# Eleven row slots for the gathered experts, and one weight buffer where there were two

## Chip, cores and metric

The kernel runs on one core of a Trainium2 chip. The metric is the device time of one launch in microseconds, the median of several runs.

## The reference

One inference step of a small diffusion backbone in float32: 384 tokens (128 of a prompt, 256 of a sample), width 1024, two layers. Layer 0 mixes tokens with an RG-LRU, layer 1 with gated linear attention (GLA); adaLN scales and shifts come from a conditioning vector. After each mixer stands PEER, a channel mixer that picks, for each token and each of 8 heads, 16 of 16384 experts by product keys, and reads from a table one row u and one row v of 1024 numbers for each:

```python
def block(args):
    xb, eb, gb = args
    ub = jnp.take(u_tab, eb, axis=0)
    act = jax.nn.gelu(jnp.einsum('td,thkd->thk', xb, ub).astype(jnp.float32))
    vb = jnp.take(v_tab, eb, axis=0)
    return jnp.einsum('thk,thkd->td', (gb * act).astype(vb.dtype), vb)
```

The GLA mixer projects each token to q, k, v, an output gate and decays (`xm @ w_in`), runs a decayed state over chunks of 64 tokens in both directions, and projects back (`@ w_out`).

## The kernel before, in words

**Order of the work.** An opening computes the adaLN vectors and the RG-LRU of layer 0. Then one long loop (`peer`, lines 1181, 776 and 1642) goes through both layers' PEER: 6 tiles of 128 tokens (prompt, sample 0, sample 1, for each layer), 8 heads each, so 48 blocks (`NBLK`) of 16 experts, and 4 steps of 4 experts per block: 192 steps (`NSLOT`). The GLA mixer of layer 1 and the expert queries of layer 1 are not a stage of their own; they run in slots beside those steps (`beside`, line 1176). The prompt's GLA begins at step 32 (`BASE[0]`) beside the tiles of the sample in layer 0, the sample's at step 96 (`BASE[1]`) beside the prompt's tile in layer 1. Each piece has a slot number written by hand; `slots.run(step)` runs what is due after the step's own work. "Step 5" of a stage is the one with slot number 5 after its `BASE`.

**One expert row.** POOL (line 441) issues an indirect DMA that gathers, for 128 tokens, one row of u and v: 8 KB for each of 128 partitions, 1.049 MB, into one of `RS` = 10 slots (`row`, line 268) in `arena`. It first waits until `row_free` says that the slot's last user is done. DVE multiplies u by the token and sums (line 1651), ACT applies gelu (L798), DVE weighs (L1662), ACT makes a diagonal matrix of the weights (L805), and PE multiplies the diagonal by v into PSUM (`pair`, line 1225, L1233) and frees two slots per pair. PE does the pairs of a step first, then parts of the expert queries of layer 0 (L1207) or the slots' mixer work. At the end of each tile (`turn`, line 1240; every 32 steps) PE waits until ACT has copied the sums out (L563), clears PSUM (L1222) and turns the tile (L1255) before it takes new rows.

**The weights.** The query weights of layer 0 (`wq0`, 8 items), the GLA weights (`gla0` for the prompt, `gla1` for the sample, 16 items each: 0 to 3 q and k, 4 to 7 v, 8 to 11 gates, 12 to 15 output) and the queries of layer 1 (`wq1`, `wq2`) are 56 items of 1 MB in the order of `ITEMS` (line 81). SP loads them one after the other (line 411) into two buffers in turn, `w_flat[0]` in `area` and `w_flat[1]` at the start of `spare` (line 264), the part of `arena` behind the ten slots. Item m is issued when PE has finished with item m - 2 (line 406). On PE, `wait_item` (line 944) waits for the item in front of the first product that needs it: `columns` (L982) for q, k, gates and output, `values` (L999) for v, `late_queries` (L1164), `queries` (L1207). An item of q and k serves two products, `q_and_k(2j)` and `q_and_k(2j+1)`. Their slots, and those of the value products (two per item in the sample's stage, one in the prompt's), are these:

```python
V_SLOTS = ((8, 9, 10, 11), (8, 9, 9, 10, 10, 11, 12, 13))
QK_SLOTS = (3, 4, 5, 6, 6, 7, 7, 8)
```

Gates stand in slots 14, 15, 18 and 19 (one item each), the output products in slots 22 to 25 (one item each, two products), and the queries of layer 1 three steps apart. The expert queries of layer 0 use one item in the first two steps of each block. SP also loads the keys of layer 1 (line 416) behind the second item of `wq1` and of `wq2`. POOL issues gathers only.

Of the kernel before, what the change touches and what calls it, by code (L numbers as in the profile page):

```python
# [13 lines left out]
D = 1024  # L14
# [20 lines left out]
PH, NK, TOPK = 8, 128, 16  # L35
NEXP = NK * NK
NB = NT * PH
RS, DS = 10, 8
HALF = P // 2
PARTS = [range(4 * i, 4 * i + 4) for i in range(4)]  # L40
NBLK = DEPTH * NB
# [4 lines left out]
AW = 3120  # L46
# [20 lines left out]
for _j in range(4, 8):  # L67
# [13 lines left out]
ITEMS = ([("wq0", h) for h in range(PH)] + [("gla0", j) for j in range(16)] + [("wq1", h) for h in range(PH)]  # L81
         + [("gla1", j) for j in range(16)] + [("wq2", h) for h in range(PH)])
ITEM_AT = {item: m for m, item in enumerate(ITEMS)}


V_SLOTS = ((8, 9, 10, 11), (8, 9, 9, 10, 10, 11, 12, 13))
# [115 lines left out]
def build(nc, x_t, pos_t, vecs, ident_d, mask_d, iota_d, keys_t, ada_w, peer_wq, peer_uv, rg_w_in,  # L202
          rg_wa, rg_wi, rg_w_out, gla_w_in, gla_w_z, w_alpha, state_gla, gla_w_out, y_t, st_rg, st_gla):
    ctx = ExitStack()
    with ctx:
# [55 lines left out]
        ada_rows = small[:, 0:512]  # L261
        gdec = small[:, 768:768 + 2 * HEADS * NCH]
        mask = sb("mask", [P, 8 * CH], U32)
        spare = arena[:, RS * 2 * D:8 * AW]
        gap = area[:, 3072:3840]

        xn1, sq1 = cols(A[0]), cols(A[2])
# [92 lines left out]
        @block.sync  # L360
        def _(sp):
            def wait_used(k):

                name, j = SEQ[k]
                if name == "ada":
                    sp.wait_ge(sem("ada_used"), j + 1)
                else:
                    sp.wait_ge(sem(name + "_mm"), 2 * j + 2)

            sources = {"rg_in": rg_w_in, "rg_out": rg_w_out}  # L370

            def stream(first, end):

                for k in range(first, end):
                    name, j = SEQ[k]
                    w = ada_w[j // 24] if name == "ada" else sources[name]
                    n = j % 24 if name == "ada" else (j + 4) % 8 if name == "rg_in" else j
                    if BEFORE[k] is not None:
                        wait_used(BEFORE[k])
                    sp.dma_start(slab_flat[SLOT[k]], w[n]).then_inc(slab_in[SLOT[k]], 16)  # L380

            def wait_item(m):

                kind, j = ITEMS[m]
                s = int(kind[-1])
                if kind[:2] == "wq":
                    sp.wait_ge(sem(f"q_mm{s}"), 2 * (j + 1))
                elif j < 4:
                    sp.wait_ge(sem("qk_mm"), 2 * j + 2 + s * BY_PROMPT["qk_mm"])
                elif j < 8:  # L390
                    sp.wait_ge(sem("v_mm"), TILES[s] * (j - 3) + s * BY_PROMPT["v_mm"])
                elif j < 12:
                    sp.wait_ge(sem("g_mm"), 2 * (j - 8) + 2 + s * BY_PROMPT["g_mm"])
                else:
                    sp.wait_ge(sem("out_mm"), 2 * (j - 12) + 2 + s * BY_PROMPT["out_mm"])

            stream(0, len(SEQ))
            wait_used(LAST_IN[SLABS])
            sp.dma_start(keys[:, :], keys_t[:, 0, :]).then_inc(keys_in, 16)
            wait_used(LAST_IN[SLABS + 1])  # L400
            sp.wait_ge(sem("rg_gate_mm"), 32)
            for m, (kind, j) in enumerate(ITEMS):
                if m == 1:
                    sp.wait_ge(sem("rg_out_mm"), C)
                elif m >= 2:
                    wait_item(m - 2)
                if kind[:2] == "wq":
                    source = peer_wq[min(int(kind[-1]), 1), j]
                else:
                    source = gla_w_in[j] if j < 12 else gla_w_out[j - 12]  # L410
                sp.dma_start(w_flat[m % 2], source).then_inc(w_in[m % 2], 16)
                if (kind, j) == ("wq0", 1):
                    sp.wait_ge(sem("rg_fin"), 1)
                    sp.dma_start(st_rg, rgfin[:, :, :]).then_inc(sem("st_rg_out"), 16)
                elif kind in ("wq1", "wq2") and j == 1:
                    sp.dma_start(keys[:, :], keys_t[:, 1, :]).then_inc(keys_in, 16)
            for i in range(4):
                sp.wait_ge(sem("y_ready"), 2 * (i + 1))
                sp.dma_start(y_t[:, 2 * i:2 * i + 2, :], hT[:, 2 * i:2 * i + 2, :]).then_inc(sem("y_out"), 16)
            sp.wait_ge(sem("y_out"), 64)  # L420
            sp.wait_ge(sem("st_rg_out"), 16)
            for i in range(2):
                sp.wait_ge(sem(f"st_gla_out{i}"), 16 * HEADS)
# [3 lines left out]
        def _(pool):  # L427
# [6 lines left out]
            for b in range(NBLK):  # L434
                pool.wait_ge(sem("idx_ready"), b + 1)
                rows = idx[b % 4]
                for j in range(TOPK):
                    n = b * TOPK + j
                    if n >= RS:
                        pool.wait_ge(row_free, n - RS + 1)  # L440
                    pool.indirect_dma_start(  # L441
                        row[n % RS], None, rows_of,
                        bass.IndirectOffsetOnAxis(ap=rows[:, j:j + 1], axis=0)).then_inc(row_in[n % RS], 16)
# [427 lines left out]
        def _(pe):  # L871
# [72 lines left out]
            def wait_item(kind, j):  # L944

                m = ITEM_AT[kind, j]
                pe.wait_ge(w_in[m % 2], 16 * (m // 2 + 1))
                return w_slab[m % 2]

            def gla(s):  # L950
                n, at, nt = WIDTH[s], BASE[s], TILES[s]
# [229 lines left out]
            def peer():  # L1181
# [17 lines left out]
                                  start=True, stop=True).then_inc(sem("first_s_mm"), 1)  # L1199

                def queries(h, half, chunks=range(C), t0=0):
                    slab_ = w_slab[h % 2]
                    if half == 0 and chunks[0] == 0:
                        wait_item("wq0", h)
                        pe.wait_ge(sem("s_ev0"), 2 * h)
# [641 lines left out]
```

## Time and profile before

| | us |
|---|---|
| median of 3 runs | 2517.98 (2516.24 to 2521.56) |
| the profiled execution | 2520.77 |
| its span | 2519.0 |
| PE busy | 1745.2 |
| DVE busy | 1540.6 |
| POOL busy | 876.5 |
| ACT busy | 647.1 |
| bytes moved | 940.29 MB, mean 373 GB/s |

The span is the time from the first to the last instruction; the execution has 1.8 us around it. Busy times of the engines overlap. Rows of the trace are quoted below in groups; in a timeline a row is a run of like instructions, with the idle time of the engine ahead of it and what ended that in brackets.

### The profile page before, as it was taken

Reading aid. Unit: us, or ns where it says so; the run is one execution under the profiler, and the core shown is the slowest. Engines: PE = TensorE matmul, PEld = TensorE weight load, DVE = VectorE, ACT = ScalarE, POOL = GpSimd, SP = SyncE. Lnnn points to the kernel's source line nnn. Section 1 sums busy time; section 2 is a strip of 40 time slices with the busy share of each in tenths; the row PEclk is TensorE's granted clock in tenths of the full one; section 3 lists DMA queues with packets and bytes.
Section 4 is the critical chain, followed back from the end, with each engine's and each line's share of the span. In section 5 each row is a group of like instructions: output and inputs, shape, how many; then the busy total and the mean of one; then the engine's idle time right before and its main releaser. Section 6 shows DMA issues by size and latency. Waiting matters only on the chain.

```text
span 2519.0 us, 28267 instructions
## 1 busy us (share of the span) xinstructions
PE 1745.2 (69%) x10284; PEld 866.4 (34%) x10284; DVE 1540.6 (61%) x3946; ACT 647.1 (26%) x1689; POOL 876.5 (35%) x775
## 2 busy tenths in 40 slices
PE   5998877765676865765665788986566765655555
PEld 2555622321343432322221455653333321211112
DVE  2225556667676766557576677765356667667753
ACT  2260312221341432221212352332112221122111
POOL 0000243534343333334444343233134444344441
PEclk8999898987788887777777799998688878677777
DMA  8883599999799999799999799989589999799994
GB/s 299 334 314 154 225 421 421 421 421 411 317 421 421 413 403 418 313 421 421 421 421 417 311 411 417 370 363 417 205 339 421 416 421 419 318 421 421 421 420 194
DMA packets 136361, 940.29 MB, mean 373 GB/s; under 512 B 19168, under 2 KB 21728, under 8 KB 22432
## 3 DMA queue, kind: packets, MB, share of 16 engines
q0 software_dynamic: 110592, 805.36, 77.6%
q1 hardware_dynamic: 17856, 126.37, 12.6%
q10 hardware_dynamic: 7776, 6.77, 0.9%
q8 instruction: 82, 1.34, 0.2%
q14 instruction: 55, 0.45, 0.0%
HBM read 935.81 MB, written 2.63 MB: 373 GB/s over the span
## 4 chain that ended last, share of the span: by engine, by line
DMA 38%; PE 35%; DVE 13%; POOL 4%; issue 4%; ACT 4%; ACTq 1%; SPq 0%; DVEq 0%
DMA arena<-in_peer_uv,idx 36%; PE psum L1233 16%; DVE arena L1651 6%; POOL arena L441 4%; PE psum L929 4%; PE psum L982 3%; PE psum L1164 2%; PE psum L1207 2%; ACT diag L805 2%; PE psum L1255 2%; PE psum L1222 2%; PE psum L894 1%; PE psum L916 1%; PE psum L1319 1%; DMA slabs<-in_ada_w 1%
## 5 line engine op out<-in xcount | busy, mean ns | idle before, releaser
L441 POOL DMA_INDIRECT arena<-in_peer_uv,idx x768 | 872.5, 1136 | 1598.1 <-PE psum L1233 1123.1
L1233 PE MATMUL psum<-arena,diag 64*64 64x512 f32 x6144 | 957.1, 775 | 651.7 <-ACT diag L805 651.6
L1651 DVE SCALAR_TENSOR_TENSOR arena<-arena,xtok 128x1024 f32<-128x1024 f32 x768 | 928.9, 1224 | 668.0 <-DMA arena<-in_peer_uv,idx 660.5
L1233 PEld LDWEIGHTS psum<-arena,diag 64*64 64x64 f32 x6144 | 303.9, 174 | 1230.3 <-issue 1228.6
L798 ACT ACTIVATE gelu<-dots 128x4 f32<-128x4 f32 x192 | 39.5, 206 | 1111.9 <-DVE arena L1651 1111.7
L805 ACT ACTIVATE diag<-ident,wts 128x64 f32<-128x64 f32 x768 | 204.3, 336 | 366.8 <-DVE wts L1662 366.8
L929 PE MATMUL psum<-arena,slabs 128*128 128x384 f32 x288 | 98.4, 502 | 9.8 <-DVE arena L1748 6.5
L798 ACT ACT_TABLE_LOAD x61 | 78.3, 1283 | 1.1
L1222 PE MATMUL psum<-zrow 1*128 1x512 f32 x48 | 40.8, 1022 | 52.0 <-ACT slabs L563 52.0
L929 PEld LDWEIGHTS psum<-arena,slabs 128*128 128x128 f32 x288 | 55.9, 196 | 49.7 <-issue 13.3
L1651 DVE DVE_READ_ACCUMULATOR arena<-arena,xtok 128x1 f32 x768 | 62.9, 82 | 0.0
L554 ACT ACT_TABLE_LOAD x45 | 57.7, 1283 | 0.8
L894 PE MATMUL psum<-slabs,cond 128*2 128x256 f32 x528 | 50.2, 401 | 9.9 <-DMA slabs<-in_ada_w 9.9
L1662 DVE TENSOR_TENSOR wts<-gelu,ex 128x4 f32<-128x4 f32 x192 | 30.5, 159 | 38.9 <-ACT gelu L798 38.9
L982 PE MATMUL psum<-area 128*128 128x128 f32 (+1 forms) x256 | 46.3, 338 | 4.2 <-DVE keys L1538 4.2
L1164 PE MATMUL psum<-area 128*128 128x128 f32 (+1 forms) x256 | 45.7, 338 | 3.0 <-ACT xtok L752 3.0
L1164 PE MATMUL psum<-area,arena 128*128 128x128 f32 (+1 forms) x256 | 46.6, 342 | 0.0
L982 PE MATMUL psum<-area,arena 128*128 128x128 f32 (+1 forms) x256 | 44.9, 331 | 0.9 <-DMA arena<-in_gla_w_in 0.9
L1255 PEld LDWEIGHTS psum<-ident,slabs 128*128 128x128 f32 x192 | 41.4, 332 | 10.5 <-issue 7.5
L1164 PEld LDWEIGHTS psum<-area 128*128 128x128 f32 x256 | 39.8, 195 | 12.9 <-issue 6.1
L1255 PE MATMUL psum<-ident,slabs 128*128 128x64 f32 x192 | 42.5, 423 | 2.1 <-ACT slabs L563 2.1
L1164 PEld LDWEIGHTS psum<-area,arena 128*128 128x128 f32 x256 | 40.5, 198 | 9.9 <-issue 6.0
(267 smaller groups left out, 1828.3 us busy)
## 6 DMA issues: line engine op xcount, KB each, us to landing
slabs<-in_ada_w SPq DMA_DIRECT2D x33, 1024.0 KB, 7.6
area<-in_peer_wq SPq DMA_DIRECT2D x12, 1024.0 KB
arena<-in_peer_wq SPq DMA_DIRECT2D x12, 1024.0 KB
arena<-in_peer_uv,idx POOLq DMA_INDIRECT x768, 11.5
area<-in_gla_w_in SPq DMA_DIRECT2D x12, 1024.0 KB
arena<-in_gla_w_in SPq DMA_DIRECT2D x12, 1024.0 KB
keys<-in_ada_w SPq DMA_DIRECT2D x8, 1024.0 KB, 8.3
area<-in_ada_w SPq DMA_DIRECT2D x7, 1024.0 KB, 7.0
```

Of the source, the lines that this page charges most:

```text
L441: pool.indirect_dma_start(row[n % RS], None, rows_of, bass.IndirectOffsetOnAxis(ap=rows[:, j:j + 1], axis=0)).then_inc(row_in[n % RS], 16)
L554: act.activation(ex[b % 4][:, :], sc[b % 4][:, :], ACT.Exp, bias=nmax[b % 4][:, 0:1], accum_out=esum[b % 4][:, 0:1]).then_inc(sem("exp_rea ...
L798: act.activation(gelu[r][:, p], dots[r][:, p], ACT.Gelu_apprx_tanh).then_inc(sem("gelu_ready"), 1)
L805: act.activation(diag[j % DS][:, :], ident2[:, :], ACT.Copy, scale=wts[r][:, j:j + 1]).then_inc(sem("diag_ready"), 1)
L894: mm = pe.matmul(out[32 * s:32 * s + 2, o:o + SW], cond[:, c, :], slab[SLOT[k]][:, c, :], start=False, stop=(c == C - 1), skip_group_check ...
L929: mm = pe.matmul(out, slab[SLOT[k]][:, c, (n % 2) * P:(n % 2 + 1) * P], rhs[:, c, :], start=(c == 0), stop=(c == C - 1))
L982: mm = pe.matmul(out[:, 0:n], slab_[:, c, (i % 2) * P:(i % 2 + 1) * P], rhs[:, c, :], start=(c == 0), stop=(c == C - 1))
L1164: mm = pe.matmul(bank[6 + half][:, 0:n], slab_[:, c, half * P:(half + 1) * P], hseg[s][:, c, :], start=(c == 0), stop=(c == C - 1))
L1222: pe.matmul(bank[i], zrow[0:1, :], zrow[0:1, 0:1].to_broadcast([1, 512]), start=True, stop=True, skip_group_check=True)
L1233: mm = pe.matmul(acc[i][o:o + HALF, half * 512:(half + 1) * 512], diag[(n + k) % DS][a:a + HALF, :], row[(n + k) % RS][a:a + HALF, D + hal ...
L1255: mm = pe.matmul(bank[4 + c // 4][:, o:o + HALF], total[:, i, c * P:(c + 1) * P], ident2[:, :], start=True, stop=True, skip_group_check=True)
L1651: ins = dve.scalar_tensor_tensor(row[n % RS][:, 0:D], row[n % RS][:, 0:D], 1.0, xtok[:, t * D:(t + 1) * D], ALU.mult, ALU.mult, accum_out= ...
```

## The change

The number of row slots goes from 10 to 11; the eleventh lies at the start of `spare`, which stays where it was, and is the same room as `w_flat[1]`. That buffer is now used once, for item 1; item 0 and all from item 2 on go through `w_flat[0]`. SP issues item 2 when PE is done with item 0, and each item m from 3 on when PE is done with item m - 1. The keys of layer 1 follow the first item of `wq1` and of `wq2`, which keeps them behind the same wait. The gather into the eleventh slot waits the first time until PE has done the queries of head 1, which read item 1.

```diff
@@ -35,7 +35,7 @@
 PH, NK, TOPK = 8, 128, 16
 NEXP = NK * NK
 NB = NT * PH
-RS, DS = 10, 8
+RS, DS = 11, 8
 HALF = P // 2
 PARTS = [range(4 * i, 4 * i + 4) for i in range(4)]
 NBLK = DEPTH * NB
@@ -81,6 +81,11 @@
 ITEMS = ([("wq0", h) for h in range(PH)] + [("gla0", j) for j in range(16)] + [("wq1", h) for h in range(PH)]
          + [("gla1", j) for j in range(16)] + [("wq2", h) for h in range(PH)])
 ITEM_AT = {item: m for m, item in enumerate(ITEMS)}
+
+
+def weight_room(m):
+
+    return (1, 1) if m == 1 else (0, max(m, 1))
 
 
 V_SLOTS = ((8, 9, 10, 11), (8, 9, 9, 10, 10, 11, 12, 13))
@@ -261,7 +266,7 @@
         ada_rows = small[:, 0:512]
         gdec = small[:, 768:768 + 2 * HEADS * NCH]
         mask = sb("mask", [P, 8 * CH], U32)
-        spare = arena[:, RS * 2 * D:8 * AW]
+        spare = arena[:, (RS - 1) * 2 * D:8 * AW]
         gap = area[:, 3072:3840]
 
         xn1, sq1 = cols(A[0]), cols(A[2])
@@ -402,17 +407,19 @@
             for m, (kind, j) in enumerate(ITEMS):
                 if m == 1:
                     sp.wait_ge(sem("rg_out_mm"), C)
-                elif m >= 2:
-                    wait_item(m - 2)
+                elif m == 2:
+                    wait_item(0)
+                elif m >= 3:
+                    wait_item(m - 1)
                 if kind[:2] == "wq":
                     source = peer_wq[min(int(kind[-1]), 1), j]
                 else:
                     source = gla_w_in[j] if j < 12 else gla_w_out[j - 12]
-                sp.dma_start(w_flat[m % 2], source).then_inc(w_in[m % 2], 16)
+                sp.dma_start(w_flat[weight_room(m)[0]], source).then_inc(w_in[weight_room(m)[0]], 16)
                 if (kind, j) == ("wq0", 1):
                     sp.wait_ge(sem("rg_fin"), 1)
                     sp.dma_start(st_rg, rgfin[:, :, :]).then_inc(sem("st_rg_out"), 16)
-                elif kind in ("wq1", "wq2") and j == 1:
+                elif kind in ("wq1", "wq2") and j == 0:
                     sp.dma_start(keys[:, :], keys_t[:, 1, :]).then_inc(keys_in, 16)
             for i in range(4):
                 sp.wait_ge(sem("y_ready"), 2 * (i + 1))
@@ -438,6 +445,8 @@
                     n = b * TOPK + j
                     if n >= RS:
                         pool.wait_ge(row_free, n - RS + 1)
+                    elif n == RS - 1:
+                        pool.wait_ge(sem("q_mm0"), 4)
                     pool.indirect_dma_start(
                         row[n % RS], None, rows_of,
                         bass.IndirectOffsetOnAxis(ap=rows[:, j:j + 1], axis=0)).then_inc(row_in[n % RS], 16)
@@ -944,8 +953,9 @@
             def wait_item(kind, j):
 
                 m = ITEM_AT[kind, j]
-                pe.wait_ge(w_in[m % 2], 16 * (m // 2 + 1))
-                return w_slab[m % 2]
+                room, fills = weight_room(m)
+                pe.wait_ge(w_in[room], 16 * fills)
+                return w_slab[room]
 
             def gla(s):
                 n, at, nt = WIDTH[s], BASE[s], TILES[s]
@@ -1199,7 +1209,7 @@
                                   start=True, stop=True).then_inc(sem("first_s_mm"), 1)
 
                 def queries(h, half, chunks=range(C), t0=0):
-                    slab_ = w_slab[h % 2]
+                    slab_ = w_slab[weight_room(ITEM_AT["wq0", h])[0]]
                     if half == 0 and chunks[0] == 0:
                         wait_item("wq0", h)
                         pe.wait_ge(sem("s_ev0"), 2 * h)
```

## Rows read from the trace of the kernel before

**Rows 1.** The page by 40 slices of 63 us: PE, DMA busy in tenths, GB/s.

```profile
PE   5998877765676865765665788986566765655555
...
DMA  8883599999799999799999799989589999799994
GB/s 299 334 314 154 225 421 421 421 421 411 317 421 421 413 403 418 313 421 421 421 421 417 311 411 417 370 363 417 205 339 421 416 421 419 318 421 421 421 420 194
```

**Rows 2.** The page's DMA queues: packets, MB, share of 16 engines; the gathers' queue.

```profile
q0 software_dynamic: 110592, 805.36, 77.6%
```

**Rows 3.** The page's costliest groups: the gathers on POOL, busy, mean, idle, releaser.

```profile
L441 POOL DMA_INDIRECT arena<-in_peer_uv,idx x768 | 872.5, 1136 | 1598.1 <-PE psum L1233 1123.1
```

**Rows 4.** Line 441 by itself: a gather from its issue to its landing.

```profile
DMA to landing us min/median/max: 5.4/11.5/21.6
```

**Rows 5.** Timeline of POOL at the first tile's end: start, us, line, [idle before].

```profile
641.77 1.18 POOL L441 DMA_INDIRECT arena<-in_peer_uv,idx  x1 [0.30 <-issue]
663.26 0.93 POOL L441 DMA_INDIRECT arena<-in_peer_uv,idx  x1 [20.32 <-PE psum L1233]
```

**Rows 6.** Table by stretch: us, busy of PE, PEld, DVE, ACT, POOL, PEclk, DMA share, GB/s.

```profile
697.00:804.00 107.00, 78.16 (x520) 45.07 (x520) 70.86 (x184) 34.78 (x86) 42.24 (x36) 0.87 1.01 420
...
1452.00:1549.00 97.00, 87.16 (x552) 56.16 (x551) 70.86 (x152) 40.59 (x81) 41.59 (x32) 0.95 1.01 418
1549.00:1660.00 111.00, 100.45 (x653) 64.77 (x655) 79.84 (x206) 38.86 (x90) 34.82 (x33) 0.95 0.92 367
```

**Rows 7.** Timeline of SP's queue, two weight loads of the first GLA stage.

```profile
726.88 0.33 SPq L411 DMA_DIRECT2D arena<-in_gla_w_in  x1
...
751.22 0.33 SPq L411 DMA_DIRECT2D arena<-in_gla_w_in  x1
```

**Rows 8.** Timeline of PE in the first GLA stage: start, us, [idle before <-releaser].

```profile
719.51 5.36 PE L1233 MATMUL psum<-arena,diag 64*64 64x512 f32 x32 [4.00 <-ACT diag L805]
...
736.16 2.02 PE L982 MATMUL psum<-area,arena 128*128 128x128 f32 x16 [0.94 <-DMA arena<-in_gla_w_in]
...
761.05 5.38 PE L999 MATMUL psum<-arena,area 128*128 128x256 f32 x16 [2.82 <-DMA arena<-in_gla_w_in]
...
794.46 3.66 PE L1233 MATMUL psum<-arena,diag 64*64 64x512 f32 x32 [2.61 <-ACT diag L805]
```

**Rows 9.** The page's DMA issues: KB each, median us to landing; loads in the opening.

```profile
area<-in_ada_w SPq DMA_DIRECT2D x7, 1024.0 KB, 7.0
```

**Rows 10.** Timeline of PE in the second GLA stage, steps 5 to 13.

```profile
1452.31 3.66 PE L1233 MATMUL psum<-arena,diag 64*64 64x512 f32 x32
1455.90 1.99 PE L992 MATMUL psum<-area 32*128 32x256 f32 x8
...
1469.78 3.62 PE L982 MATMUL psum<-area 128*128 128x256 f32 x16
1475.55 3.66 PE L1233 MATMUL psum<-arena,diag 64*64 64x512 f32 x32 [2.15 <-ACT diag L805]
1479.14 3.72 PE L982 MATMUL psum<-area 128*128 128x256 f32 x16
...
1489.77 6.57 PE L1233 MATMUL psum<-arena,diag 64*64 64x512 f32 x32 [3.45 <-ACT diag L805]
...
1499.83 3.62 PE L999 MATMUL psum<-area 128*128 128x256 f32 x16
...
1531.92 1.47 PE L1009 MATMUL psum<-ident,keys 128*128 128x128 f32 x12
...
1545.88 3.41 PE L1020 MATMUL psum<-xtok,slabs 128*64 128x64 f32 x64
1549.21 3.66 PE L1233 MATMUL psum<-arena,diag 64*64 64x512 f32 x32
```

**Rows 11.** Timeline of PE at the second stage's output projection.

```profile
1677.57 7.17 PE L982 MATMUL psum<-slabs,area 128*128 128x256 f32 x32
...
1732.62 6.32 PE L1233 MATMUL psum<-arena,diag 64*64 64x512 f32 x32 [11.26 <-ACT diag L805]
```

## The prediction

> **What bounds the kernel now.** I read the page by slices first. From the sixth slice on the DMA line sits at 421 GB/s, and falls below it in a few places [rows 1]. 421 is the most that any slice shows, so I take it as full. Nearly all of the traffic is the 768 gathers of expert rows: 805.36 MB, so 1.049 MB or 2.49 us each at 421 GB/s [rows 2]. Until the end the kernel is as fast as gathers can be issued, and a gather is issued when PE has freed a slot: POOL's idle time ahead of the gathers is put down to PE's L1233 for 1123.1 us [rows 3]. A gather lands 5.4 us after its issue at the least and 11.5 in the median [rows 4]; the 6.1 us between are queueing, and they say how late PE can free a slot before the DMA engines run dry.
>
> The dips are of two kinds. Five of them (slices 11, 17, 23, 29 to 30, 35) are the ends of token tiles: POOL's timeline at the first shows the issues stopping at 641.77 and starting again at 663.26, after 20.32 us of waiting for PE [rows 5]; the slots are full and PE is in the turn. The others belong to the GLA stages, in which PE has the mixer's products besides the rows. The table of stretches [rows 6] has the first stage's busiest part (697 to 804 us, 420 GB/s, PE busy 78 of 107 us) and the second's: in 1452 to 1549 DMA is still full (418 GB/s) but PE is busy for 87.16 of 97 us, and in 1549 to 1660 PE (100.45 of 111 us) has become the limit, at 367 GB/s. In the second stage there is no room on PE. That is where this change is decided.
>
> **The change, part by part.** A step is four rows on PE, 32 recorded products, 3.66 us at full clock [rows 10], and then that step's share of the mixer, all in one order on one engine.
>
> *The eleventh slot, gains.* At a turn the slots run full and DMA waits; one more gather in them is 2.49 us less of waiting. Five turns: 12.5 us. Inside a stretch that PE limits, the slot lets DMA run 2.49 us further before it stops, once per stretch: the slack of 6.1 us becomes 8.6. The eleventh gather now waits for the queries of head 1 in place of the first freed row; DMA is full there and nothing is lost.
>
> *One buffer for the weights, costs.* The load of item m now starts when PE has finished with item m-1, not m-2. What a load takes is seen where PE already waits for one: SP issues at 726.88 and 751.22 [rows 7], the products that need them start at 736.16 and 761.05 behind a wait for that DMA [rows 8]: 9.28 and 9.83 us. I take 9.3. The gathers are issued as the step's rows are freed, so a load issued some 4 us later always shares the engines with them, as those two did. From below I bound it by 7.0, the median of loads of this size in the opening, where no gathers run [rows 9], from above by 9.8. The Trainium skill, in "DMA: Bandwidth & Descriptors", section "Anatomy of one DMA — SWDGE (gpsimd) path", gives about 2.0 us plus the bytes over 436 GB/s for a transfer on the gathers' path, an estimate of 4.4 us here and, put into the working below, of +3.5 us for the whole change. The two loads above took over twice that, and the rows decide.
>
> PE also runs slowly after a wait: the sixteen products that waited 2.82 us for their weights took 5.38 us [rows 8], and the same form took 3.62 with no wait ahead, and rows after 3.45 us of idle time took 6.57 instead of 3.66 [rows 10]. The stretches' clock lies between half and all of 2.4 GHz [rows 6], and such rows are at the 1.2 GHz level for a part of them. I charge 1.8 us per wait; ends 0 and 2.9.
>
> *Second GLA stage, q, k and v (steps 5 to 12).* By the slots in the code, q_and_k(3) and q_and_k(4) stand in one step and use different items, and so do 5 and 6, then 7 and the first values, then values 1 and 2, then 3 and 4. Each of these five steps must now hold a whole load: rows 3.66 + product 3.72 + wait 9.3 + product 3.62 + slow clock 1.8 = 22.1 us [rows 10]. Step 5 has rows 3.66 and decays 1.99 between its two items, so it waits 3.65 and lasts 14.8; step 11 has no new item (3.66 + 3.72 + 1.47 = 8.85); in step 12 the transposes of step 11, the rows and 0.5 of transposes stand between, so it waits 3.7 and with its attention (3.41) lasts 16.7. Together 14.8 + 110.5 + 8.85 + 16.7 = 150.9 us. Before, the same eight steps went from 1452.31 to 1549.21, 96.9 us. PE comes out 54.0 us later. Nothing covers it: what follows is limited by PE as well [rows 6], so only the new slot's 2.5 is got back. **+51.5.** PE's in-order queue puts the next rows behind each wait, so freeing, gathers, dots and diags all follow it; ACT's and DVE's shares of the mixer fall into these waits and cost nothing.
>
> *Second stage, output projection.* Four items in four steps of rows and two products of 3.58 each (7.17 together) [rows 11]. Between two items stand only the rows, so three steps wait 5.6 and last 3.66 + 5.6 + 7.17 + 1.8 = 18.3. DMA needs five transfers of 2.49 per step, 12.45. Three times 5.85 is 17.5, less 8.6 of slack: **+8.9.** (In the rows before, DMA was the limit after it: 11.26 us of idle at 1732.62.)
>
> *First stage.* Products of 2.0 instead of 3.7 [rows 8]. Steps 6 and 7: 3.66 + 2.0 + 9.3 + 2.0 + 1.8 = 18.8 each; step 8, with the first values: 20.4; steps 9 to 11, one item each, wait 5.6 behind their rows: 14.7 each, and 1.0 of transposes. Sum 103.1 us against 75.0 before (719.51 to 794.46). Of these 28.1 the slack takes 8.6, since DMA is full there and PE had idle time after it: **+19.5.** Its later items (gates, outputs) wait 4 to 6 us at a time; the idle time that PE has after them covers that, and if it does not they cost 2 us each.
>
> *Elsewhere.* Items of the expert queries have two or three whole steps (20 us and more) between the end of one and the start of the next, against 9.3: nothing. The keys are issued behind the same release as before. If that cover were gone, each would cost its 9.3.
>
> **Sum:** 51.5 + 8.9 + 19.5 - 12.5 = +67.4 us. The profiled execution took 2520.77 (span 2519.0 and 1.8 around it), 2.8 above the median of the runs. 2520.8 + 67.4 - 2.8 = 2585.
>
> **Rivals.** *A, the loads are short.* With DMA less full a load may land as the fastest gather does, 5.4 us for the same megabyte [rows 4]. The five steps then last 18.2, the eight steps 120.4 (+23.5), the first stage and the output projection come within the slack: 23.5 - 2.5 - 12.5 = +8.5, 2526. The skill's estimate above points this way. For it: DMA will be idle for part of these steps. Against: four gathers stand ahead of each load in every one of them. 9 in 100.
> *B, faster.* The rows already in the slots carry the pipeline over PE's waits, so that only the turns' gain is left: 2518 - 12.5 = 2505. This decides when PE's lateness in a stage stays below 8.6 us; for it, at 736.16 and 761.05 PE waited and DMA stayed full [rows 6, 8]. Against it stands the second stage, where PE has only 9.8 of 97 us idle [rows 6] for five waits. 5 in 100.
> *C, the slot does not do what it should*, because the gathers' pace is set in groups of four rows and the odd one never runs ahead: the 12.5, 2.5 and two times 2.5 are lost, +20, 2605. 6 in 100.
>
> **How the numbers follow.** The forecast has 80 in 100. A load of 7.0 takes 2.3 from each of the sixteen waits (7, 3 and 6 by stage), 37 us less, 2548; one of 9.8 adds 8. The clock's ends are 29 less and 18 more. Not all go one way, so 2545 to 2612; this holds C, and leaves out A and B and some of the forecast's tails. A measurement can tell about 0.2% (5 us) from no change: within it lies the near edge of A and B, 0.05; faster 0.05; slower 0.90.
>
> **What would show it.** In PE's timeline of the second stage, waits of some 9 us for the DMA of the weights inside five successive steps; those steps near 22 us; DMA there near 60 to 70%; the turns' gaps shorter by about 2.5. It is wrong if these waits are near 5 us, if PE's time between the rows of step 5 and step 13 grows by less than 35 us, or if DMA stays at 418 GB/s through that stretch.

## The result and the profile after

The changed kernel takes 2582.99 us in the median of 4 runs (2574.95 to 2587.0), the kernel before 2517.24 (4 runs): a ratio of 1.0246, 95% interval 1.0221 to 1.027, or 56 to 68 us slower. The profiled execution has a span of 2585.2 us against 2519.0.

The page of the changed kernel, its slices and three of its costliest groups:

```profile
PE   4999877665757766766656756978476665665555
...
DMA  7884599999889999899998956989679999899994
GB/s 272 321 317 164 229 421 421 421 421 409 339 356 362 421 421 416 337 421 421 421 421 331 417 226 266 397 331 380 279 282 421 421 421 421 342 422 421 421 421 196
...
L450 POOL DMA_INDIRECT arena<-in_peer_uv,idx x768 | 875.7, 1140 | 1659.8 <-PE psum L1243 1158.5
...
L992 PE MATMUL psum<-area 128*128 128x128 f32 (+1 forms) x512 | 106.8, 374 | 57.1 <-DMA area<-in_gla_w_in 53.0
...
L1009 PE MATMUL psum<-area 128*128 128x256 f32 x192 | 60.9, 487 | 56.4 <-DMA area<-in_gla_w_in 56.4
```

Busy times are those of before to within a few us; what has grown is idle time. In [rows 1] the 12th and 13th slices stood at 421 GB/s and now stand at 356 and 362; where the second GLA stage runs there are now two slices at 226 and 266, the lowest of the PEER loop but for its last slice. The two groups of the mixer's products (L992 was L982, L1009 was L999) are behind the weights' DMA. The table of waits puts a sum to that; engine and line, what it waited for, us in total, times, longest:

```profile
PE psum L1009 <- DMA area<-in_gla_w_in: 56.4, 8, 10.2
PE psum L992 <- DMA area<-in_gla_w_in: 53.0, 7, 9.8
```

The stretches that answer to [rows 6], with the same columns:

```profile
722.00:824.00 102.00, 60.17 (x344) 37.66 (x343) 54.10 (x130) 30.55 (x67) 27.12 (x24) 0.77 0.86 348
...
1464.00:1621.00 157.00, 100.22 (x549) 65.35 (x548) 75.93 (x170) 42.31 (x83) 37.39 (x32) 0.78 0.69 276
1621.00:1738.00 117.00, 100.18 (x668) 64.80 (x670) 85.83 (x209) 42.16 (x94) 40.70 (x36) 0.95 0.92 369
```

The columns behind POOL's are the granted clock of PE as a share of 2.4 GHz, the busy share of the DMA engines and GB/s. The second stage's steps 5 to 12 take 157 us with DMA 69% in use, 276 GB/s; the stretch behind them is as it was, 369 GB/s. The timeline of PE shows where the time lies; rows that answer to [rows 10], from the rows of step 5 to those of step 13:

```profile
1464.23 3.66 PE L1243 MATMUL psum<-arena,diag 64*64 64x512 f32 x32
...
1473.39 5.38 PE L992 MATMUL psum<-area 128*128 128x256 f32 x16 [3.57 <-DMA area<-in_gla_w_in]
...
1495.74 6.19 PE L992 MATMUL psum<-area 128*128 128x256 f32 x16 [9.73 <-DMA area<-in_gla_w_in]
...
1518.86 6.58 PE L992 MATMUL psum<-area 128*128 128x256 f32 x16 [9.68 <-DMA area<-in_gla_w_in]
...
1542.49 6.70 PE L1009 MATMUL psum<-area 128*128 128x256 f32 x16 [9.81 <-DMA area<-in_gla_w_in]
...
1566.60 6.60 PE L1009 MATMUL psum<-area 128*128 128x256 f32 x16 [10.16 <-DMA area<-in_gla_w_in]
...
1590.18 5.07 PE L1009 MATMUL psum<-area 128*128 128x256 f32 x16 [9.74 <-DMA area<-in_gla_w_in]
...
1612.07 6.06 PE L1009 MATMUL psum<-area 128*128 128x256 f32 x16 [4.08 <-DMA area<-in_gla_w_in]
...
1621.39 3.66 PE L1243 MATMUL psum<-arena,diag 64*64 64x512 f32 x32
```

Five waits of 9.68 to 10.16 us stand in five successive steps, a shorter one ahead and one behind. Each ends with the DMA of the weights, and each product that waited is slow: 5.07 to 6.70 us for what takes 3.62 to 3.72 with no wait. The five steps last 22.0 to 24.0 us, from rows to rows.

A part of the difference of the two spans has nothing to do with the change. The first gather, before and after, in POOL's timelines:

```profile
281.40 1.08 POOL L441 DMA_INDIRECT arena<-in_peer_uv,idx  x1 [276.86 <-DVE flag L1466]
```

```profile
288.16 1.08 POOL L450 DMA_INDIRECT arena<-in_peer_uv,idx  x1 [283.63 <-DVE flag L1476]
```

It comes 6.8 us later, and nothing ahead of it was changed. In all fourteen profiles of this study it came between 278.6 and 289.4 us, and the same kernel had it at 286.8 and at 279.5 in two profiles. So where two profiles are compared below, the time from the first gather to the end is used: 2237.6 us before, 2297.0 after, 59.4 more; 54.1 more in a second profile of the changed kernel. The other end moves too: from PE's rows of the last step to the end of the span the fourteen profiles take 26.3 to 32.3 us, in no order that follows the kernels.

### The profile page after: what moved, and what is told of

It is laid out like the page before. It is cut to its first block, busy times and chain, and to the rows that moved or that the text cites. A ratio compares the mean times of both kernels' runs of the same rounds, so it can differ in the third digit from the quotient of the medians.

```text
span 2585.2 us, 28267 instructions
## 1 busy us (share of the span) xinstructions
PE 1747.4 (68%) x10284; PEld 884.1 (34%) x10284; DVE 1539.4 (60%) x3946; ACT 649.3 (25%) x1689; POOL 879.7 (34%) x775
## 4 chain that ended last, share of the span: by engine, by line
DMA 42%; PE 35%; DVE 14%; ACT 3%; issue 3%; POOL 2%; ACTq 1%; SPq 0%; DVEq 0%; POOLq 0%
DMA arena<-in_peer_uv,idx 34%; PE psum L1243 11%; PE psum L992 6%; DVE arena L1661 5%; DMA area<-in_gla_w_in 5%; PE psum L938 4%; PE psum L1009 2%; POOL arena L450 2%; PE psum L1174 2%; DMA area<-in_gla_w_out 2%; PE psum L1265 2%; PE psum L1232 2%; ACT diag L814 1%; PE psum L1217 1%; PE psum L903 1%
## 5 line engine op out<-in xcount | busy, mean ns | idle before, releaser
L1243 PE MATMUL psum<-arena,diag 64*64 64x512 f32 x6144 | 920.3, 748 | 578.1 <-ACT diag L814 578.0
L1243 PEld LDWEIGHTS psum<-arena,diag 64*64 64x64 f32 x6144 | 291.8, 168 | 1131.0 <-issue 1128.7
L992 PE MATMUL psum<-area 128*128 128x128 f32 (+1 forms) x512 | 106.8, 374 | 57.1 <-DMA area<-in_gla_w_in 53.0
L992 PEld LDWEIGHTS psum<-area 128*128 128x128 f32 x512 | 91.2, 224 | 76.2 <-issue 62.7
L1009 PE MATMUL psum<-area 128*128 128x256 f32 x192 | 60.9, 487 | 56.4 <-DMA area<-in_gla_w_in 56.4
L1174 PE MATMUL psum<-area 128*128 128x128 f32 (+1 forms) x512 | 91.9, 339 | 3.1 <-ACT xtok L761 3.1
L1174 PEld LDWEIGHTS psum<-area 128*128 128x128 f32 x512 | 80.0, 197 | 22.7 <-issue 12.1
L1217 PE MATMUL psum<-area 128*128 128x384 f32 (+1 forms) x224 | 79.5, 503 | 1.8 <-ACT area L501 1.8
L938 PEld LDWEIGHTS psum<-arena,slabs 128*128 128x128 f32 x288 | 55.9, 197 | 49.9 <-issue 13.6
L1009 PEld LDWEIGHTS psum<-area 128*128 128x128 f32 x192 | 47.1, 252 | 72.9 <-issue 63.7
L1217 PEld LDWEIGHTS psum<-area 128*128 128x128 f32 x224 | 43.0, 201 | 46.5 <-issue 25.3
L903 PE MATMUL psum<-slabs,cond 128*2 128x256 f32 x528 | 49.1, 393 | 9.5 <-DMA slabs<-in_ada_w 9.5
```

Of the source, the lines that this page charges most:

```text
L903: mm = pe.matmul(out[32 * s:32 * s + 2, o:o + SW], cond[:, c, :], slab[SLOT[k]][:, c, :], start=False, stop=(c == C - 1), skip_group_check ...
L938: mm = pe.matmul(out, slab[SLOT[k]][:, c, (n % 2) * P:(n % 2 + 1) * P], rhs[:, c, :], start=(c == 0), stop=(c == C - 1))
L992: mm = pe.matmul(out[:, 0:n], slab_[:, c, (i % 2) * P:(i % 2 + 1) * P], rhs[:, c, :], start=(c == 0), stop=(c == C - 1))
L1009: mm = pe.matmul(out[:, 0:SW], hseg[s][:, c, t * P:(t + 1) * P], slab_[:, c, :], start=(c == 0), stop=(c == C - 1))
L1174: mm = pe.matmul(bank[6 + half][:, 0:n], slab_[:, c, half * P:(half + 1) * P], hseg[s][:, c, :], start=(c == 0), stop=(c == C - 1))
L1217: mm = pe.matmul(bank[6 + half][:, t0 * P:T], slab_[:, c, half * P:(half + 1) * P], hP[:, c, t0 * P:T], start=(c == 0), stop=(c == C - 1))
```

## The experiments

The theory: PE's in-order queue takes the load's whole time as a wait wherever an item is used up and the next one begun in one step; the eleventh slot gives back some 2.5 us where DMA runs dry. The rivals: the slot is worth nothing; late loads cost alike wherever they are; the waits are about bytes.

**One buffer with ten slots.** The rule for the buffers was made a list, with the waits worked out from it (the next two kernels have other rules):

```diff
+def room_rule(m):
+    return 1 if m == 1 else 0
...
-                    wait_item(m - 2)
+                    wait_item(LAST_USER[m])
...
-                sp.dma_start(w_flat[m % 2], source).then_inc(w_in[m % 2], 16)
+                sp.dma_start(w_flat[ROOM[m]], source).then_inc(w_in[ROOM[m]], 16)
```

> Ten row slots as before, and the single weight buffer of the change (item 1 alone in the second). Theory (PE's waits for the loads cost some 77 us, the eleventh slot gives back some 11 at the turns and some 2.5 in each of three stretches that PE limits): slower than the changed kernel, 2583 + 11 to 18 us, about 2597; the turns' gaps in DMA are back to 10 to 12 us. Rival (the slot does nothing, or costs): 2583 or less, with the turns' gaps as in the changed kernel.

Measured: 2599.28 us, 1.0295 of before (1.0272 to 1.0319; before was at 2527.03 on that chip). Beside the 1.0246 of the changed kernel that leaves 0.0049, some 12 us, for the slot (the two intervals just miss each other); by the traces from the first gather on it is 2313.9 - 2297.0 = 16.9, and 21.3 up to PE's rows of the last step. By the gaps of over 0.3 us between DMA packets of over 1 KB in the traces the engines stand idle at the first, second, third and fifth turn for 11.0, 12.2, 11.5 and 9.8 us before, 8.1, 10.1, 9.5 and 8.1 with the change, and 10.4, 12.0, 10.8 and 7.2 here. The first three are back. At the fifth nothing can be read: its gap is 7.2 to 9.8 us in the four profiles of kernels with ten slots. The fourth has a gap of 17.1 us before, 14.3 with the change and 15.6 here. The third is the cleanest. Its longest gap, all packets counted, is 9.86 us in all four profiles with ten slots, 7.35 to 7.41 in the eight with eleven, and 4.88 and 4.91 in the two with twelve (a run below): one gather of 2.49 us for each slot. The slot does what it was taken to do.

**One buffer in the second stage alone, and in the first alone.** With ten slots, and the rule's one line changed, first for the second stage:

```diff
...
+    return m % 2 if m < ITEM_AT["gla1", 0] else 0
...
```

> Ten row slots; two buffers in turn as before up to the first GLA stage and the prompt's queries, one buffer from the second GLA stage (sample) on. Theory: nearly all of the loss sits there, since PE has no idle time: before + 60 to 66 us, about 2580, with five waits of 9.5 to 10 us in five successive steps. Rival (each late load costs alike, wherever it is): the second stage has 10 of 16 longer waits, so some 45 us, about 2562.

Measured: 2583.24 us, 1.0234 (1.0211 to 1.0257), 53 to 65 us more. PE's timeline has the same picture:

```profile
1478.33 6.17 PE L992 MATMUL psum<-area 128*128 128x256 f32 x16 [9.53 <-DMA area<-in_gla_w_in]
...
1501.51 6.53 PE L992 MATMUL psum<-area 128*128 128x256 f32 x16 [9.76 <-DMA area<-in_gla_w_in]
...
1525.31 6.57 PE L1009 MATMUL psum<-area 128*128 128x256 f32 x16 [10.03 <-DMA area<-in_gla_w_in]
...
1549.37 6.49 PE L1009 MATMUL psum<-area 128*128 128x256 f32 x16 [10.24 <-DMA area<-in_gla_w_in]
...
1573.15 6.54 PE L1009 MATMUL psum<-area 128*128 128x256 f32 x16 [10.05 <-DMA area<-in_gla_w_in]
```

Then for the first:

```diff
...
+    return 0 if ITEM_AT["gla0", 0] <= m < ITEM_AT["wq1", 0] else m % 2
...
```

> Ten row slots; one buffer in the first GLA stage (prompt) alone, two in turn elsewhere. Theory: PE comes out of steps 6 to 11 some 28 us late, and all but the slack of about 6 us is lost: before + 16 to 24 us, about 2537. Rival (each late load costs alike): 6 of 16 waits, about 27 us or more, 2545. A second rival (idle time on PE later in the stage takes it up): within 5 us of before.

Measured: 2540.72 us, 1.0067 (1.0036 to 1.0098), 9 to 25 us more. PE waits as long here, 9.24 to 11.00 us three times in the first rows of the stage:

```profile
742.96 3.75 PE L992 MATMUL psum<-area 128*128 128x128 f32 x16 [9.24 <-DMA area<-in_gla_w_in]
...
762.89 3.75 PE L992 MATMUL psum<-area 128*128 128x128 f32 x16 [10.07 <-DMA area<-in_gla_w_in]
...
784.01 6.01 PE L1009 MATMUL psum<-area 128*128 128x256 f32 x16 [11.00 <-DMA area<-in_gla_w_in]
```

Yet the loss is under a third of the second stage's. The two add up, 2.34% and 0.67% against 2.95% for both. That late loads cost alike wherever they are is out: with 10 and 6 of the 16 waits the stages would have shared the loss 63 to 37, and they share it 78 to 22 by the times, 74 to 26 by the two profiles from the first gather on (62.6 and 22.2 us).

**A slot that is shared with the second weight buffer.** Both GLA stages have two buffers again. Outside of them the second buffer's room is the eleventh slot; a list says which slot each row has and which row it follows there:

```diff
+SHARED = ((RS - 1, 140), (244, 396), (500, NBLK * TOPK))
...
+    return 1 if m == 1 else m % 2 if ITEMS[m][0][:3] == "gla" else 0
...
+                if kind[:3] == "gla" and j == 1:
+                    sp.wait_ge(row_free, SHARED_END[int(kind[-1])] + 1)
...
-                        pool.wait_ge(row_free, n - RS + 1)
+                    elif PRIOR[n] >= 0:
+                        pool.wait_ge(row_free, PRIOR[n] + 1)
```

> Two weight buffers in turn during both GLA stages, one outside of them; the second buffer's room is the eleventh row slot for rows 10 to 139, 244 to 395 and from 500 on, that is at all five turns. Theory (the slot is worth some 2.3 us at each turn and the waits come from the single buffer in the stages): before - 11 us, about 2506, no new waits of PE for weights. Rival (the slot does nothing by itself): 2517. Second rival (handing the room over costs waits of its own on POOL or SP): above 2520.

Measured: 2503.45 us, 0.9917 of before (0.9894 to 0.994), 15 to 27 us less where 11 were expected. A second time, beside the next kernel:

> The kernel with the shared eleventh slot once more, beside the one with two shared slots on one chip. Theory: 0.992 to 0.994 of before (17 us less in its profile from the first gather on, where the opening's own time is left out). Rival: within 0.2% of before.

2503.51 us, 0.9938 (0.9915 to 0.996). From the first gather on the two profiles are 17.0 and 19.6 us shorter than before, and 15.4 and 13.6 up to PE's rows of the last step. Not all of this is the slot's. At PE's rows of the fifth step, ahead of every turn, 2.9 and 2.8 us of it are there; the kernel with ten slots and one buffer has 3.1 us there too, and the two kernels that keep two buffers for the expert queries of layer 0 have 0.3 and 0.5. So this part comes with the single buffer for those queries. What is left, 12.5 and 10.8 us, is what five turns of 2.49 us give.

**A twelfth slot** in the room that the stages use for values and states, for the same rows, with a wait for `row_free` ahead of those rooms' first writers (against the kernel with the shared eleventh slot):

```diff
-RS, DS = 11, 8
+RS, DS = 12, 8
...
-SHARED = ((RS - 1, 140), (244, 396), (500, NBLK * TOPK))
+SHARED = ((RS - 2, 140), (244, 396), (500, NBLK * TOPK))
...
```

> As the kernel with the shared eleventh slot, and a twelfth slot, in the room that the GLA stages use for values and states, for the same rows. Theory (each slot is worth some 2.5 us at each turn while DMA still runs dry there, 8 to 13 us in the kernel with eleven): another 12 to 17 us, 0.977 to 0.981 of before if the eleventh's 0.992 holds... that is 0.985 to 0.987 of before; at the turns DMA is idle for 5 to 11 us. Rival (past eleven the slots do not bind, PE's turn or the index does): the same as with eleven, 0.992.

Measured: 2491.88 us, 0.989 (0.9858 to 0.9923), above what was expected, with an interval that overlaps the eleven-slot kernel's. (In the expectation 0.985 to 0.987 is what is meant; the pair of numbers ahead of it is a slip.) Both were run again on one chip:

> The kernel with two shared slots once more. Theory: another 14 us below the one with one shared slot (the difference of the two profiles from the first gather on), 0.986 to 0.989 of before. Rival (the twelfth slot adds nothing that can be measured): the two within 5 us of each other.

2485.83 us, 0.9869 (0.9841 to 0.9897), 17.7 us below the 2503.51 of its neighbour, and the two intervals do not overlap. From the first gather on the profiles differ by 13.8 us here and by 13.9 in the first pair. POOL's timeline at the first tile's end, with eleven and with twelve slots:

```profile
638.00 0.94 POOL L479 DMA_INDIRECT arena<-in_peer_uv,idx  x1 [0.30 <-issue]
657.74 1.45 POOL L479 DMA_INDIRECT arena<-in_peer_uv,idx  x1 [18.80 <-PE psum L1271]
```

```profile
637.59 0.94 POOL L482 DMA_INDIRECT arena<-in_peer_uv,idx  x1 [0.30 <-issue]
657.09 1.40 POOL L482 DMA_INDIRECT arena<-in_peer_uv,idx  x1 [18.55 <-PE psum L1276]
```

POOL still waits there, as in [rows 5], but the DMA engines are idle for 8.9 and 6.3 us in place of 11.0. This is the fastest kernel of the study: the idea of the change, with the single buffer kept out of the two stages that pay for it.

**Half of each load.** How much of the wait is bytes? The loads of the second stage brought half of their columns; this kernel and the next leave out a part of the sample's mixer, and only their times count:

```diff
...
+                part = slice(0, C * SW // 2 if kind == "gla1" and j >= 2 else C * SW)
...
```

> The changed kernel, but from the third item of the second GLA stage on each load brings only the first half of its columns (14 loads of 0.5 MB); the second half of the weights is left as it was, so the sample's mixer is not computed. Theory (a late load costs its start behind the gathers, about 3.4 us, and its bytes at half of the engines' rate, about 5 us): the five waits shrink from 9.8 to about 7.1 us, and the stage gains some 2.7 us in seven waits and some in the output projection, about 20 us in all: 25 to 15 us faster than the changed kernel. Rival (a late load waits until the four gathers ahead of it are through, whatever its size): waits stay above 9 us and the gain is under 10 us. Second rival (the fixed part is small, bytes are all): waits near 5.5 us, 35 us faster.

Measured: 2566.73 us, 1.0192 (1.0157 to 1.0226). The waits, two of the five:

```profile
1482.90 5.31 PE L993 MATMUL psum<-area 128*128 128x256 f32 x16 [8.48 <-DMA area<-in_gla_w_in]
...
1504.11 6.64 PE L993 MATMUL psum<-area 128*128 128x256 f32 x16 [8.65 <-DMA area<-in_gla_w_in]
```

They lie between 8.48 and 9.21 us, not at 7.1: of 9.5 to 10.2 us half of the bytes is worth about one. The theory's split into a start and bytes fails. By the medians the kernel is some 13 us faster than the changed one on that chip, with intervals that overlap; its waits are shorter by about 1 us each, and DMA has 14 times 0.5 MB less to move (17 us at 421 GB/s). The packets had stayed as many, so the next kernel halved their number:

```diff
...
+                part = slice(0, HALF if kind == "gla1" and j >= 2 else P)
...
```

> Half loads again (14 loads of 0.5 MB from the third item of the second GLA stage on, the rest of the weights left as it was, the sample's mixer not computed), but by partitions 0 to 63 with rows of 8 KB, half as many packets of full size, where the run before had as many packets of half size and waits of 8.5 to 9.2 us. Theory (on each DMA engine a load's packets take turns with the gathers' one by one, 8 of them at 0.31 us each beside 0.31 us of gather): four turns fewer, 2.5 us less, waits of 7.0 to 7.6 us in the five steps. Rival (the load ends when the gathers ahead of it are through, whatever it holds): 8.5 us and more, as there.

Measured: 2578.98 us, 1.0228 (1.0196 to 1.026), not to be told from the change (1.023 in its second run).

```profile
1492.55 6.11 PE L993 MATMUL psum<-area 128*128 128x256 f32 x16 [9.84 <-DMA area<-in_gla_w_in]
...
1515.46 6.59 PE L993 MATMUL psum<-area 128*128 128x256 f32 x16 [9.56 <-DMA area<-in_gla_w_in]
...
1559.77 6.62 PE L1010 MATMUL psum<-area 128*128 128x256 f32 x16 [8.46 <-DMA area<-in_gla_w_in]
```

Four of five waits are 9.56 to 9.85 us. That theory is out as well. But the trace's 8 KB packets of these loads took 0.47 to 0.60 us in the median instead of 0.31, so this half was also a slower one, and the two cannot be told apart here. What is left is the contrast inside the changed kernel. In the second stage's steps 5 to 12 a load takes 9.05 to 10.13 us from its issue until PE starts, and its first packet comes 2.7 to 3.7 us after the issue. One of the output projection's, behind whose issue only the last eight packets of a gather still start, has its first packet after 0.97 us; SP's row, and PE's rows that answer to [rows 11]:

```profile
1768.44 0.33 SPq L418 DMA_DIRECT2D area<-in_gla_w_out  x1
```

```profile
1743.93 7.17 PE L992 MATMUL psum<-slabs,area 128*128 128x256 f32 x32
...
1758.96 9.45 PE L992 MATMUL psum<-slabs,area 128*128 128x256 f32 x32 [4.25 <-DMA area<-in_gla_w_out]
...
1773.37 7.14 PE L992 MATMUL psum<-slabs,area 128*128 128x256 f32 x32 [1.36 <-DMA area<-in_gla_w_out]
...
1787.76 8.71 PE L992 MATMUL psum<-slabs,area 128*128 128x256 f32 x32 [3.65 <-DMA area<-in_gla_w_out]
...
1802.88 3.66 PE L1243 MATMUL psum<-arena,diag 64*64 64x512 f32 x32 [2.81 <-ACT diag L814]
```

From 1768.44 to 1773.37 are 4.93 us, for the same megabyte. A load of the first stage that is issued at 784.80, when no gather is under way, has its first packet after 0.97 us and its product at 789.80, 5.00 us after the issue. The packets show where the rest goes. The load issued at 1486.04, behind which PE waits 9.73 us, has its first packet 3.52 us after the issue and its last ends at 9.15; the one at 1768.44 has 0.97 and 4.47. So of the 4.7 us between them 2.5 are a later start, in which packets of the gathers run alone, and 2.1 a slower run, in which packets of the gathers start between its own.

**PE kept at work ahead of the waits.** Why are the products behind a wait slow? Ahead of each of the five, PE did products into the bank that is then overwritten:

```diff
+                def awake(out):
+                    for c in range(2 * C):
+                        pe.matmul(out[:, 0:n], ones[:, :], hseg[s][:, c % C, :], start=True, stop=True,
+                                  skip_group_check=True)
...
+                    if s and name in ("qk4", "qk6"):
+                        awake(out)
...
+                    if s and i in (0, 2, 4):
+                        awake(out)
...
```

> The changed kernel, and ahead of each of the five waits in the second GLA stage PE does sixteen products of 256 columns into the bank that the waiting product then overwrites, some 7.2 us of work that nothing needs. Theory (PE's products after a wait are slow because PE stood idle, some 2.6 us each time, beside the wait itself): the products after the five waits take 3.6 to 4 us in place of 5.1 to 6.7, what is left of the waits is 2 to 3 us, and the kernel is 10 to 14 us faster. Rival (the slow products come from reading weights that have just landed, or from the DMA traffic): they stay at 5 to 6.7 us and the time stays within 4 us.

Measured: 2578.86 us, 1.0231 (1.0203 to 1.0259), not to be told from the change by time. Two of five products were fast, three slow; one of each:

```profile
1496.19 3.72 PE L1000 MATMUL psum<-area 128*128 128x256 f32 x16 [2.75 <-DMA area<-in_gla_w_in]
...
1517.52 5.41 PE L1000 MATMUL psum<-area 128*128 128x256 f32 x16 [3.46 <-DMA area<-in_gla_w_in]
```

2.1 to 3.5 us of idle time were left ahead of them, so the work was made longer (`range(20)`):

> As the run in which PE works ahead of the five waits, with twenty products in place of sixteen, some 8.8 us, so that under 1.5 us of each wait is left idle (2.1 to 3.5 us were left, and three of the five products behind them still took 5.4 to 6.8 us, the other two 3.7). Theory (idle time ahead of it makes a product slow): all five take 3.6 to 4 us, rows of step 5 to rows of step 13 in 143 to 147 us (156.5 and 157.2 in the two profiles of the changed kernel, 152.2 with sixteen). Rival (weights that have just landed, or traffic, make it slow): again three or more of five at over 5 us, 151 us or more.

Measured: 2572.42 us, 1.0213 (1.0177 to 1.025). In the timeline the four products with 0.51 to 1.17 us of idle time ahead took 3.72 us, and the one with 2.09 took 5.41:

```profile
1457.28 3.66 PE L1254 MATMUL psum<-arena,diag 64*64 64x512 f32 x32
...
1488.94 3.72 PE L1000 MATMUL psum<-area 128*128 128x256 f32 x16 [1.17 <-DMA area<-in_gla_w_in]
...
1510.63 5.41 PE L1000 MATMUL psum<-area 128*128 128x256 f32 x16 [2.09 <-DMA area<-in_gla_w_in]
...
1553.52 3.72 PE L1020 MATMUL psum<-area 128*128 128x256 f32 x16 [1.09 <-DMA area<-in_gla_w_in]
...
1603.71 3.66 PE L1254 MATMUL psum<-arena,diag 64*64 64x512 f32 x32
```

From step 5 to step 13 PE takes 146.4 us instead of 156.5 in the second profile of the change. The granted clock of these stretches, the change first:

```profile
1461.00:1618.00 157.00, 99.86 (x558) 65.45 (x560) 76.34 (x170) 42.39 (x83) 37.59 (x32) 0.79 0.70 278
```

```profile
1457.00:1604.00 147.00, 133.34 (x758) 96.26 (x760) 76.67 (x171) 42.30 (x83) 38.00 (x32) 0.95 0.74 298
```

It is 0.79 of 2.4 GHz when PE stands idle in the waits and 0.95 when it works through them. Over the products alone it is 0.54 to 0.72 for the five that take 5.07 to 6.70 us in the changed kernel's first profile, 1.00 for the four that take 3.72 here and 0.68 for the one of 5.41. All of these read weights that have just landed, and the DMA engines are busy for 0.08 to 0.36 of the time during the products of 3.72 us and for 0.00 to 0.19 during the longer ones. So the slow products are at the 1.2 GHz level for a part of their time because PE stood idle, and not because of the weights or the traffic. The interval of the time is too wide to show those 10 us.

**The changed kernel again**, on the chip of the half loads:

> The changed kernel once more, for the comparison on one chip: 1.022 to 1.027 of before. The first gather starts 281 to 291 us after the span's start whatever the kernel, since nothing in the opening was changed; a difference of some 7 us between two profiles there is the opening's own.

2579.49 us, 1.023 (1.0195 to 1.0265), its first gather at 288.2 us.

## Why the prediction was right, step by step

The forecast was 2585 us and 2583 were measured. The mechanism is the one that was forecast, but the closeness is luck, as the table shows. The places where PE's rows stand in the two profiles let each term be read off. The opening's 6.8 us come first; then the lateness against before:

| up to | before | after | late by | step's own | predicted |
|---|---|---|---|---|---|
| the first gather | 281.40 | 288.16 | 6.8 | +6.8 | 0 |
| first stage, rows of step 6 [rows 8] | 719.51 | 721.89 | 2.4 | -4.4 | -2.5 |
| first stage, rows of step 12 | 794.46 | 824.06 | 29.6 | +27.2 | +28.1 |
| second stage, rows of step 5 [rows 10] | 1452.31 | 1464.23 | 11.9 | -17.7 | -13.6 |
| second stage, rows of step 13 | 1549.21 | 1621.39 | 72.2 | +60.3 | +54.0 |
| output projection, first item [rows 11] | 1677.57 | 1743.93 | 66.4 | -5.8 | -2.5 |
| rows behind the output projection | 1732.62 | 1802.88 | 70.3 | +3.9 | +8.9 |
| end of the span | 2519.0 | 2585.2 | 66.2 | -4.1 | -5.0 |

From the first gather on the profiles differ by 59.4 us (54.1 in the second profile of the change), and 67.4 were forecast. The second stage cost 6.3 us more than its term, the output projection 5.0 less, and the other stretches together 9.3 less. In these profiles the later opening, which was in no term, fills most of the gap of 8 us; what fills it in the medians, 65.8 us apart, no run shows.

For the first stage, PE's rows in the timeline of the changed kernel:

```profile
721.89 5.36 PE L1243 MATMUL psum<-arena,diag 64*64 64x512 f32 x32 [4.31 <-ACT diag L814]
...
738.63 3.75 PE L992 MATMUL psum<-area 128*128 128x128 f32 x16 [9.40 <-DMA area<-in_gla_w_in]
...
758.12 3.75 PE L992 MATMUL psum<-area 128*128 128x128 f32 x16 [9.82 <-DMA area<-in_gla_w_in]
...
778.23 6.54 PE L1009 MATMUL psum<-area 128*128 128x256 f32 x16 [9.95 <-DMA area<-in_gla_w_in]
...
789.80 3.69 PE L1009 MATMUL psum<-area 128*128 128x256 f32 x16 [1.43 <-DMA area<-in_gla_w_in]
...
824.06 3.66 PE L1243 MATMUL psum<-arena,diag 64*64 64x512 f32 x32
```

- *A load takes 9.3 us from issue to product.* It took 9.05 to 10.13 in the second stage and 9.37 to 9.92 at the three long waits of the first; a little more than forecast. The bound of 7.0 from below was too high: with next to no gathers under way two loads took 4.93 and 5.00. The second stage came out 60.3 us late instead of 54.0: the five long waits make 2.6 of the difference (49.1 in sum against 46.5), and slower products most of the rest.
- *1.8 us of slow clock per wait.* In the second stage it was 1.4 to 3.1, nearer the upper end that was kept for the range. The last pair of runs shows that the mechanism was the right one.
- *The first stage comes out 28.1 us late.* It did so by 27.2, with errors that cancel: its three long steps last 20.4, 19.5 and 22.9 us where 18.8, 18.8 and 20.4 were summed, and step 9 lasts 8.7 in place of 14.7, since its load, issued at 784.80, found no gathers and PE waited 1.43 us in place of 5.6.
- *The output projection loses 5.6 us per step.* Here the size was off: waits of 4.25, 1.36 and 3.65 us. An item's two products last 7 to 9 us here, and a load meets fewer gathers: behind the first and the third their packets run for 3 us and are then nearly through, behind the second almost none start. 3.9 us were lost in place of 8.9.
- *Slack takes 8.6 us of the first stage's lateness.* More was won back, 17.7 with two turns against 13.6. The two kernels with ten slots and one buffer in that stage, whose turns give nothing, come out of it 24.7 and 26.7 us late and win back 5.5 and 4.3 up to the second stage, near the 6.1 that the prediction has for ten slots. So the slack was about right and most of the lateness stays; it is the slot that gave 12 to 13 us in this stretch in place of 7.5.
- *The slot gives 12.5 us at the turns and 2.5 per stretch.* Summed that is 20. With one buffer it is worth 12 by the times and 16.9 by the traces (21.3 up to the rows of the last step); with two buffers in the GLA stages it is worth 10.8 and 12.5 up to those rows.
- *Rival A (short loads)* fell with the waits of 9.7 us and more, although DMA was at 69%. The Trainium skill's fit for transfers on the gathers' path ("DMA: Bandwidth & Descriptors", "Anatomy of one DMA — SWDGE (gpsimd) path"), 4.4 us for this size as an estimate, is near the 4.93 and 5.00 us of the two loads on SP's queue that met almost no gathers, and half of what the loads of the long waits took. *Rival B (rows in the slots carry the pipeline)* holds in part behind the first stage, where 17.7 us are won back, and not behind the second. *Rival C (the slot does nothing)* fell with the runs of ten, eleven and twelve slots.

What was not tried: eleven slots with two full buffers in all of the run, for which `arena` has no room as it is laid out; and a wait shortened by sending the gathers later than the load.

## What to carry to other kernels

Before two buffers are made one, look in the timeline for places where one item is used up and the next begun with nothing between: each will hold a whole load, at the price of a load behind the traffic that runs there, not of one by itself. The same wait costs less where the engine that waits has idle time to give, here some 3 to 4 us each in the first stage against 6 in the second, so count by stage. And room that two users need at different times can be given to both, which here turned a loss of 2.5% into a gain of 0.6 to 0.8% with one shared slot and of 1.1 to 1.3% with two.

## What was not expected of the hardware

- A load behind the gathers took 8.4 to 10.1 us until its product whether it brought 1 MB, half the columns or half the partitions, and 4.93 and 5.00 us when next to no gathers were under way.
- PE's products were slow behind 2.09 us of idle time and not behind 1.17; behind 2.75 and 3.02 us they were fast in two cases, so the length of the idle time alone does not decide.
- The first gather came at 278.6 to 281.4 us in eight profiles and at 286.8 to 289.4 in six, for the same opening.
